# Router logits and expert gathers as float32 products of unsplit x, in a two-layer encoder kernel on one core

## What is computed

```python
for l in range(2):
    x = layer_norm(ALPHA * x + hybrid_mixer(x, ...), ln1_g[l], ln1_b[l])
    ffn = swiglu(x, ...) if l == 0 else moe_swiglu(x, router_w[0], router_b[0], ...)
    x = layer_norm(ALPHA * x + ffn, ln2_g[l], ln2_b[l])

def moe_swiglu(x, router_w, router_b, wg, wu, wd):
    logits = x @ router_w + router_b             # (256, 8)
    top_logit, top_idx = lax.top_k(logits, 2)
    top_w = softmax(top_logit)
    # each expert e: rows of the tokens that chose it, silu(xb@wg[e])*(xb@wu[e]) @ wd[e], times their weight,
    # added back to the tokens
```

## Time and profile before

| | |
|---|---|
| median of 3 runs | 1084.34 us (1083.81 to 1087.44) |
| the profiled execution | 1084.33 us, its span 1082.5 us |
| PE busy | 1049.4 us, 97% of the span |
| DVE busy | 662.6 us, 61% |
| ACT busy | 535.1 us, 49% |
| POOL busy | 90.1 us, 8% |
| mean granted clock of PE over the span | 0.988 of 2.4 GHz |
| moved by DMA | 343.28 MB, mean 317 GB/s |

### The profile page before, as it was taken

The page is one execution under the profiler, slowest core; times in us unless marked ns, Lnnn a source line. Parts: engine busy times, 40 slices in busy tenths (PEclk is TensorE's granted clock), DMA queues, the critical chain, the costliest instruction groups (busy, mean ns, idle before and its releaser), DMA issues.

```text
span 1082.5 us, 15639 instructions
## 1 busy us (share of the span) xinstructions
PE 1049.4 (97%) x6164; PEld 805.5 (74%) x6164; DVE 662.6 (61%) x912; ACT 535.1 (49%) x814; POOL 90.1 (8%) x101
## 2 busy tenths in 40 slices
PE   8998999999899999999999999999999999999995
PEld 7976888888799788886657886557887557887562
DVE  6878645545668789982039884119975109986104
ACT  5674534444357657771047772128764108765102
POOL 0002000000100039930000000000000000000002
PEclk9998999999999999999999999999999999999997
DMA  9933655454262419998999999999999999999991
GB/s 381 405 110 140 252 180 200 184 194 176 99 232 103 159 61 381 371 377 352 421 421 421 421 421 376 423 420 420 422 420 376 422 420 421 421 420 377 420 417 46
DMA packets 48012, 343.28 MB, mean 317 GB/s; under 512 B 5360, under 2 KB 5488, under 8 KB 6592
## 3 DMA queue, kind: packets, MB, share of 16 engines
q1 hardware_dynamic: 46656, 336.09, 76.8%
q0 software_dynamic: 992, 5.56, 1.5%
q10 hardware_dynamic: 288, 0.59, 0.1%
HBM read 341.17 MB, written 1.05 MB: 316 GB/s over the span
## 4 chain that ended last, share of the span: by engine, by line
PE 86%; DVE 7%; ACT 4%; issue 1%; DMA 1%; DVEq 0%; ACTq 0%
PE bank L816 14%; PE bank L566 13%; PE bank L568 12%; PE bank L567 12%; PE bank L807 6%; PE bank L718 6%; PE bank L721 6%; PE bank L724 6%; PE bank L793 3%; DVE wlo L1599 2%; PE bank L560 1%; PE bank L739 1%; PE bank L880 1%; PE bank L798 1%; ACT whi L971 1%
## 5 line engine op out<-in xcount | busy, mean ns | idle before, releaser
L1599 DVE TENSOR_TENSOR wlo<-raw,whi 128x1024 fp32r<-128x1024 f32 x260 | 306.4, 1231 | 18.8 <-ACT whi L1152 17.7
L1152 ACT ACTIVATE whi<-raw 128x1024 fp32r<-128x1024 f32 x260 | 255.9, 1052 | 2.4 <-PE bank L568 2.4
L568 PE MATMUL bank<-whi,al 128*128 128x512 f32 (+1 forms) x624 | 234.6, 376 | 0.0
L816 PE MATMUL bank<-raw,xg 128*64 128x256 f32 x1408 | 161.6, 380 | 0.0
L1277 DVE TENSOR_TENSOR wlo<-raw,whi 128x1024 fp32r<-128x1024 f32 x110 | 130.4, 1221 | 27.2 <-ACT whi L971 26.4
L1651 DVE TENSOR_TENSOR he<-he,bank 128x128 f32<-128x128 f32 x44 | 12.7, 288 | 219.2 <-ACT he L1207 219.2
L566 PE MATMUL bank<-whi,xgh 128*128 128x512 f32 x352 | 142.5, 405 | 3.3 <-DVE wlo L1599 2.9
L567 PE MATMUL bank<-wlo,xgh 128*128 128x512 f32 x352 | 137.1, 389 | 0.0
L568 PEld LDWEIGHTS bank<-whi,al 128*128 128x128 f32 x624 | 118.2, 189 | 22.1
L816 PEld LDWEIGHTS bank<-raw,xg 128*64 128x64 f32 x1408 | 98.5, 137 | 46.0 <-issue 2.2
L971 ACT ACTIVATE whi<-raw 128x1024 fp32r<-128x1024 f32 x114 | 115.3, 1057 | 23.1 <-PE bank L568 17.4
(11 more groups left out here) (283 smaller groups left out, 1360.2 us busy)
## 6 DMA issues: line engine op xcount, KB each, us to landing
raw<-W SPq DMA_DIRECT2D x319, 1024.0 KB, 11.4
scr<-gb_d POOLq DMA_DIRECT2D x3, 1024.0 KB, 5.0
scr<-wbd_d POOLq DMA_DIRECT2D x2, 512.0 KB, 6.2
x<-gb_d POOLq DMA_DIRECT2D x1, 1024.0 KB, 9.3
out_d<-acc SPq DMA_DIRECT2D x4, 256.0 KB, 2.0
x<-x_d SPq DMA_DIRECT2D x1, 512.0 KB, 4.2
x<-x_d ACTq DMA_DIRECT2D x1, 512.0 KB, 7.8
rtab<-rt_d POOLq DMA_DIRECT2D x1, 228.0 KB, 2.8
```

The lines of the kernel that those rows point to most:

```text
L568: return nc.tensor.matmul(out, sl, mh, start=False, stop=last, skip_group_check=True)
L816: last = nc.tensor.matmul(bank[n * NARROW:(n + 1) * NARROW, c % 2, 0:FC].rearrange("p (a n) -> p a n", a=2), xg[:, kk, :], gu[:, :, n * P: ...
L1152: nc.scalar.activation(whi[:, q % SPLIT, h * HW:(h + 1) * HW], raw[:, i % RING, h * HW:(h + 1) * HW], ACT.Copy).then_inc(hi_rdy, 1)
L1599: V.tensor_tensor(wlo[:, q % SPLIT, h * HW:(h + 1) * HW], raw[:, i % RING, h * HW:(h + 1) * HW], whi[:, q % SPLIT, h * HW:(h + 1) * HW].bi ...
```

## The change

The parts of the split x give way to one unsplit, transposed copy `xT`, and the logits of a tile are 8 float32 products of it with the router's weights (128 tokens stationary, 8 columns moving). They come out with tokens on partitions, so that the copy to ACT and the two small transposes go away. The logits of tile 0 are made between the two tiles' transposes. Gathers are products of x itself and a float32 `S`, two for a block instead of four. ACT and DVE share the copies to `xT`: ACT three of the four half-tiles, DVE the second half of tile 1. The split of the router's weights goes. The counts' two products move behind the fillers ahead of the gather, into bank 2, with a semaphore of their own that DVE awaits in `tables`. The four one-hot instructions become one. `gbx` gets its own buffer. The fillers are 3, 4, 7, 3, 7 and 3 (27) in place of 18, 20, 9, 10 and 5 (62).

```diff
-WARM = {... "last_mixer": 18, "tile": 20, "split": 9, "rank": 10, "slots": 5}
+WARM = {... "last_mixer": 3, "tile": 4, "tile2": 7, "split": 3, "rank": 7, "slots": 3}
...
-        S = sb("S", [P, NT, P], F32R)
+        S = sb("S", [P, NT, P])
+        xT = sb("xT", [P, KT, T])
-        xnh = sb("xnh", [P, NT, D], F32R)
-        xnl = sb("xnl", [P, NT, D], F32R)
+        gbx = sb("gbx", [P, 2, D])
...
             def gather(b, m):
-                    for n, (t, a) in enumerate(((0, xnh), (0, xnl), (1, xnh), (1, xnl))):
-                        last = nc.tensor.matmul(bank[:, 4 + b, k * P:k * P + m], a[:, t, kk * P:(kk + 1) * P],
-                                                S[:, t, 0:m], start=(n == 0), stop=(n == 3))
+                    for t in range(NT):
+                        last = nc.tensor.matmul(bank[:, 4 + b, k * P:k * P + m], x[:, t, kk * P:(kk + 1) * P],
+                                                S[:, t, 0:m], start=(t == 0), stop=(t == NT - 1))
...
             def router():
+                def logits(t):
+                    for g in range(2):
+                        if t == 1 and g == 1:
+                            pe.wait_ge(xTb_rdy, 1)
+                        else:
+                            pe.wait_ge(xTa_rdy, 2 * t + g + 1)
+                        for k in range(4 * g, 4 * g + 4):
+                            last = nc.tensor.matmul(bank[:, 3, (3 + t) * NE:(4 + t) * NE], xT[:, k, t * P:(t + 1) * P],
+                                                    rw[:, k * NE:(k + 1) * NE], start=k == 0, stop=k == KT - 1)
+                    last.then_inc(lg_ps, 1)
+
                 keep_warm(WARM["last_mixer"], 6)
                 transpose_x(3, 0)
-                keep_warm(WARM["tile"], 6, htl[:, :, :].rearrange("p t n -> p (t n)"))
+                pe.wait_ge(rt_in, 16)
+                keep_warm(WARM["tile"], 3, idle)
+                logits(0)
+                keep_warm(WARM["tile2"], 6, idle)
                 transpose_x(3, 1)
-                keep_warm(WARM["split"], 3, htl[:, :, :].rearrange("p t n -> p (t n)"))
-                split_ready(3, 1, 1)
-                pe.wait_ge(rw_l, 1)
-                for k in range(KT):
-                    nc.tensor.matmul(bank[0:2 * NE, 2, 0:T], rw2[:, k].rearrange("p a e -> p (a e)"), xTh[:, k, :], ...)
-                    last = nc.tensor.matmul(bank[0:NE, 2, 0:T], rw2[:, k, 0, :], xTl[:, k, :], ...)
-                last.then_inc(lgT_ps, 1)
-                pe.wait_ge(lgT_sb, 1)
-                for t in range(NT):
-                    nc.tensor.transpose(bank[:, 3, ...], lgs[0:2 * NE, t * P:(t + 1) * P], ...).then_inc(lg_ps, 1)
+                keep_warm(WARM["split"], 4, idle)
+                logits(1)
                 keep_warm(WARM["rank"], 4)
                 pe.wait_ge(mk_rdy, 1)
...
-                nc.tensor.matmul(bank[:, 3, 2 * NE:3 * NE], ones, mk[:, 0, :], start=True, stop=False)
-                nc.tensor.matmul(bank[:, 3, 2 * NE:3 * NE], ones, mk[:, 1, :], start=False,
-                                 stop=True).then_inc(pos_ps, 1)
                 keep_warm(WARM["slots"], 4)
+                nc.tensor.matmul(bank[:, 2, 0:NE], ones, mk[:, 0, :], start=True, stop=False)
+                nc.tensor.matmul(bank[:, 2, 0:NE], ones, mk[:, 1, :], start=False, stop=True).then_inc(cnt_ps, 1)
...
# ACT, std(2)
-                        act.wait_ge(x_rdy, 2 * (2 * NT + t + 1))
-                        nc.scalar.activation(xnh[:, t, :], x[:, t, :], ACT.Copy).then_inc(xn_h, 1)
+                        for g in range(2 - t):
+                            act.wait_ge(xT_ps, 12 + 2 * t + g + 1)
+                            nc.scalar.activation(xT[:, 4 * g:4 * g + 4, t * P:(t + 1) * P], bank[:, xbank(t, g), :]...,
+                                                 ACT.Copy).then_inc(xTa_rdy, 1)
...
# DVE, norm(2)
-                if ph == 2:
-                    split_x(ph + 1, 0)
-                split_x(ph + 1, 1)
-                if ph == 2:
-                    for t in range(NT):
-                        low_x(t)
+                if ph < 2:
+                    split_x(ph + 1, 1)
+                else:
+                    copy_x(1)
...
-            for a in range(2):
-                for t in range(NT):
-                    chain.mark(V.tensor_scalar(oh[:, a, t, :], iota[:, 0:NE], ixf[:, t, a:a + 1], None, ALU.is_equal))
-            chain.settle()
+            link(V.tensor_tensor(oh[:], ids, picks, ALU.is_equal))
...
             def tables():
-                link(V.tensor_copy(cnt, bank[:, 3, 2 * NE:3 * NE]))
+                dve.wait_ge(cnt_ps, 1)
+                link(V.tensor_copy(cnt, bank[:, 2, 0:NE]))
```

More of the change, by code:

```diff
@@ L92, in piece_of @@
     return CLASSES[J], J // 2, i
-WARM = {"start": 8, "mixer": 2, "dense": 12, "last_mixer": 18, "tile": 20, "split": 9, "rank": 10, "slots": 5}
+WARM = {"start": 8, "mixer": 2, "dense": 12, "last_mixer": 3, "tile": 4, "tile2": 7, "split": 3, "rank": 7,
+        "slots": 3}
 POOL_PIECES = (MIXP + 1, MIXP + FFP + 1)
@@ L202, in build @@
         rb = rtab[:, 3 * P + KT * NE:]
-        rw2 = hth[:, 0, 0:KT * 2 * NE].rearrange("p (k a e) -> p k a e", k=KT, a=2)
         def small(first, n, pat=None, **kw):
@@ L207, in small @@
             return r.rearrange(pat, **kw) if pat else r
-        lgs = he
         lg = small(0, 16, "p (t e) -> p t e", t=NT)
@@ L239, in build @@
         y32 = raw[:, RING - 1, 0:D]
-        gbx = x[:, :, :]
         bank = ctx.enter_context(nc.psum_tensor("bank", [P, 8, 512], F32))
@@ L283, in build @@
         y0_ps = sem("y0_ps")
-        rw_h = sem("rw_h")
-        rw_l = sem("rw_l")
+        xTa_rdy = sem("xTa_rdy")
+        xTb_rdy = sem("xTb_rdy")
         yh_sb = sem("yh_sb")
-        xn_h = sem("xn_h")
-        xn_l = sem("xn_l")
         acc0_rdy = sem("acc0_rdy")
@@ L309, in build @@
         hTl_rdy = sem("hTl_rdy")
-        lgT_ps = sem("lgT_ps")
-        lgT_sb = sem("lgT_sb")
         lg_ps = sem("lg_ps")
@@ L318, in build @@
         cnt_rdy = sem("cnt_rdy")
+        cnt_ps = sem("cnt_ps")
         pool_step = sem("pool_step")
@@ L835, in between @@
                     for t in range(NT):
-                        last = nc.tensor.transpose(bank[0:n, 7, t * P:(t + 1) * P], S[:, t, 0:n].bitcast(F32), ident[:])
+                        last = nc.tensor.transpose(bank[0:n, 7, t * P:(t + 1) * P], S[:, t, 0:n], ident[:])
                     last.then_inc(st_ps, 1)
@@ L903, in router @@
             def router():
+                def logits(t):
[8 more added lines that the diff above has]
+                    last.then_inc(lg_ps, 1)
+                idle = htl[:, :, :].rearrange("p t n -> p (t n)")
                 keep_warm(WARM["last_mixer"], 6)
                 transpose_x(3, 0)
-                keep_warm(WARM["tile"], 6, htl[:, :, :].rearrange("p t n -> p (t n)"))
+                pe.wait_ge(rt_in, 16)
+                keep_warm(WARM["tile"], 3, idle)
+                logits(0)
+                keep_warm(WARM["tile2"], 6, idle)
                 transpose_x(3, 1)
-                keep_warm(WARM["split"], 3, htl[:, :, :].rearrange("p t n -> p (t n)"))
-                split_ready(3, 1, 1)
-                pe.wait_ge(rw_l, 1)
-                for k in range(KT):
[L913 to L916, removed]
-                last.then_inc(lgT_ps, 1)
-                pe.wait_ge(lgT_sb, 1)
-                for t in range(NT):
-                    nc.tensor.transpose(bank[:, 3, 3 * NE + 2 * t * NE:3 * NE + 2 * (t + 1) * NE],
-                                        lgs[0:2 * NE, t * P:(t + 1) * P], ident[0:2 * NE, 0:2 * NE]).then_inc(lg_ps, 1)
+                keep_warm(WARM["split"], 4, idle)
+                logits(1)
                 keep_warm(WARM["rank"], 4)
@@ L926, in router @@
                 nc.tensor.matmul(bank[:, 3, NE:2 * NE], ones, mk[:, 0, :], start=True, stop=False)
-                nc.tensor.matmul(bank[:, 3, NE:2 * NE], tri, mk[:, 1, :], start=False, stop=True)
-                nc.tensor.matmul(bank[:, 3, 2 * NE:3 * NE], ones, mk[:, 0, :], start=True, stop=False)
-                nc.tensor.matmul(bank[:, 3, 2 * NE:3 * NE], ones, mk[:, 1, :], start=False,
-                                 stop=True).then_inc(pos_ps, 1)
+                nc.tensor.matmul(bank[:, 3, NE:2 * NE], tri, mk[:, 1, :], start=False, stop=True).then_inc(pos_ps, 1)
                 keep_warm(WARM["slots"], 4)
+                nc.tensor.matmul(bank[:, 2, 0:NE], ones, mk[:, 0, :], start=True, stop=False)
+                nc.tensor.matmul(bank[:, 2, 0:NE], ones, mk[:, 1, :], start=False, stop=True).then_inc(cnt_ps, 1)
             mixer(0)
@@ L937, in _ @@
             pe.wait_ge(S_rdy, 1)
-            pe.wait_ge(xn_l, 2)
             gather(0, WIDE)
@@ L991, in std @@
                     nc.scalar.activation(rstd[:, t:t + 1], mv[:, t, 1:2], ACT.Sqrt).then_inc(std_rdy, 1)
-                    if split:
+                    if split and ph < 2:
                         split_x(ph + 1, t)
```

(29 more changed lines are left out.)

## The result

| | before | changed |
|---|---|---|
| median | 1084.07 us (4 runs) | 1077.35 us (4 runs, 1076.49 to 1079.03) |
| ratio | | 0.9933, 95% interval 0.9917 to 0.9948 |
| again, on one chip (five rounds) | 1084.43 us | 1077.29 us, ratio 0.9940 (0.9926 to 0.9953) |
| the profiled execution | 1084.33 us, span 1082.5 us | 1079.03 us, span 1077.2 us |

Of all runs told here, five took 1325 to 2131 us instead of some 1080 (two of the kernel before, one of it with the split early, two of the last experiment); they are left out of the ratios and ranges.

The account below looks back on a forecast made before the run. TensorE, busy 97%, was taken as the bound, with the router set by VectorE's chain, small products and TensorE's clock. 1084.33 - 3.27 (path) + 1.26 (clock) = 1082.3 us; range 1080.4 to 1086.5.

Parts of the forecast that it names:

- The splits: Router: splits of x, router's weights and rows lie beside other work; taking them away gains nothing more.
- The fillers: Router: the fillers on TensorE are padding, paced by VectorE; they fall from 62 to 27.
- The path from the second tile to the gather: Router, second tile's transposes to the gather's first weights: 389.64 instead of 392.91, 3.27 us earlier.
- The clock: Router: TensorE's granted clock falls near 377 and returns by 380.5, costing 1.26 us; chance 0.36.
- The gap of 3.24 us: Router: TensorE idle from the end of 3 fillers near 373.6 until the first transposes at 376.84.
- rival A: Router: the clock stays up, -3.27 us, 1081.1 us; chance 0.27.
- rival B: Router: clock returns only after the first tile's logits and 7 fillers; cost 4.63, net +1.4, 1085.7 us; chance 0.19.
- the early end: Router: of 380.5 to 383.8 us for the clock's return after a fall near 377, 380.5 was taken.
- Rival C: Router: thin work keeps the clock low until the expert; cost 14.4, net +11.1, 1095.5 us; chance 0.09.
- The gathers: Gather products: 16 float32 products of two records, 32 records at 0.111 us again, 3.55 us, no change.
- The price by the rule of passes: Gathers: four passes per float32 product would double 3.5 us for each of eight pairs of halves, 28 us in all.
- The counts' wait: VectorE, ahead of the weights' chain: 389.92 instead of 389.41; costs nothing now, 0.5 us without the queue's cover.

Follow-up runs that it names:

- the last experiment: Changed kernel with 14 fillers instead of 2 after the first mixer and 12 ahead of the tail's branch: 1075.28 to 1076.58 us, ratio 0.9918 to before.

## Why the prediction was wrong, step by step

**The splits.** "Lie beside other work today, and taking them away gains nothing more": this step failed. True of the splits of x and of the rows; false of the split of the router's weights, which stood ahead of the normalisation on VectorE with an idle time of 4.06 us in its own row. The prediction began its reading with the second tile's rows at 383.04 and took them as given ("this stays"). They came 4.1 us earlier. The run that puts the split back and the one that moves it up in the kernel before show it from both sides.

**The fillers.** "The fillers there are padding" was half of it. They were sized to end when the rows came, so that they would have kept most of the gain; that the change also cuts them is a part of the gain (1083.27 against 1079.56 us in the kernel before). The prediction costed their cut only as a risk for the clock.

**The path from the second tile to the gather.** Right: 3.27 us, by 6.6 us from the rows to the gather. Its steps hold too, counted from the second tile's rows: the mask reached TensorE 4.80 us after them (4.81 forecast), VectorE went on 5.74 after them (5.76), and the logits' records came 0.11 us apart, as taken.

**The clock.** The gap of 3.24 us on which the forecast of 1.26 us rested never came about, since the transposes were no longer late; in that sense rival A was right on the clock for another reason. Where the gap was made to come back in the changed kernel, the clock stayed low for 10.2 us and the price was about 5.3 us, not 1.26: of its own cases rival B (4.63 us) was the one that such a gap brings, and taking "the early end, since transposes, fillers and products follow closely" was wrong. Rival C's mechanism, thin work that doesn't bring the clock back until the expert, showed only with no fillers at all, at 5 us and not 11.

**The gathers.** Right in kind: records of 0.114 instead of 0.110 us in the first gather, +0.55 us over the run by the chain, +1.1 by the medians, where 0 was taken. (The price by the rule of passes was itself summed short: the chain shows nine gathers, the first and eight pairs of halves, so nearly 32 us and not 28.) The Trainium skill's four passes for a float32 product (FP8 and Floating Point Precision, TensorE Precision Notes) didn't decide: both forms were held at the pace of their weight loads, 0.11 us apart. At 256 columns this case's trace agrees with it: a float32 product's two records of 0.216 us make 4.05 cycles a column at 2.4 GHz.

**The counts' wait.** VectorE waited 0.37 us for them, where 0.5 was worked out, and nothing came of it.

Together: 4.1 (wait) + 3.3 (path) - 0.6 (gathers) = 6.8 us; measured 6.7 and 7.1. The medians of the kernel before alone lie 0.6 us apart (1084.07 to 1084.68), so an agreement to 0.1 us is partly luck. The forecast's 1.26 us for the clock is no part of it: its gap did not occur.

## What to carry to other kernels

When a change takes an instruction away, look first at the idle time in its own row and at what is queued behind it on its engine: a copy of 0.2 us that waits for a neighbour's queue can hold up the longest chain of the stage, and it shows neither in busy time nor in the chain of waits if filler products stand on TensorE meanwhile. Fillers that end just when the data comes are no proof that the data sets the time; take the wait away and they are the next bound, so size them again after every change ahead of them. And where a gap of some 3 us is left on TensorE, expect the clock to fall, and look at what stands behind it: here 11 dense products that other work covered cost nothing, 4 of them with thin products behind cost 5 us. Filling the gap itself kept the clock up after the first mixer.

## What the runs showed of the hardware

A fall of TensorE's clock after the same gap of 3.16 us was over by 382.0, some 3.4 us later, with 11 products of 512 columns behind it, and lasted 10.2 us with 4 such products, 16 records of 8 columns and 7 more such products. Each is one trace, and the 6.8 us after the first mixer, with dense products from 97.1 us on, shows that dense work doesn't always bring it back as soon. Products issued ahead of a branch on a loaded register ran while TensorE's sequencer took it: 12 of them used up the 2.7 us for which the engine had been idle there, and the next product came 0.2 us later than without them (2.9 us after the last expert product's end, instead of 2.7).
